# Modulation sums as f32 column-tile products with a block transpose on VectorE, and products of constants on TensorE ahead of the attention's first head

## The chip, the cores and the metric

The kernel runs on one core of a Trainium2 chip. The metric is the device time of one execution in microseconds (us). A difference under 0.3% can't be told from no change in this kernel.

## What is computed

The program is a decoder trunk of two layers over 512 tokens of 1024 channels. A conditioning vector gives nine modulation vectors per layer (a shift, a scale and a gate for each of three sublayers), and these come from a product of one row with a 1024 by 9216 matrix per layer:

```python
e = jax.nn.silu(c @ cond_w + cond_b[None, :])
for i in range(DEPTH):
    mod = (e @ ada_w[i] + ada_b[i][None, :]).reshape(B, N_SUBLAYERS, N_MOD, D_MODEL)
    shift, scale, gate = mod[:, :, 0], mod[:, :, 1], 1 + mod[:, :, 2]
    h = modulate(x, norm_g[i, 0], shift[:, 0], scale[:, 0])
    x = x + 0.5 * gate[:, 0][:, None, :] * swiglu(h, ffn_w1[i, 0], ffn_w3[i, 0], ffn_w2[i, 0])
    ...        # the mixer: a causal convolution in layer 0, stick-breaking attention in layer 1
    h = modulate(x, norm_g[i, 2], shift[:, 2], scale[:, 2])
    x = x + 0.5 * gate[:, 2][:, None, :] * swiglu(h, ffn_w1[i, 1], ffn_w3[i, 1], ffn_w2[i, 1])
```

The attention has 16 heads of 64 channels. For each head it forms logits z, a softplus of z, a sum of that over later keys, and the exponential of the difference as the weight of a value.

## The kernel before

Five engines run their own programs, written out by hand with semaphores between them. Nothing is scheduled by a planner, so the order of an engine is the order of its code. Channels lie on the 128 partitions, tokens along the free axis. A large product is exact to f32 by a split: each operand is a high part in fp32r and the low rest, and `triple` multiplies high by high, high by low and low by high (three TensorE products of 128x512). Weights arrive by DMA (issued by SyncE) in `raw`, ScalarE writes their high part to `w`, VectorE the low part, and TensorE waits on `lo_done` for each slab.

A feed-forward sublayer (`ffn`, four of them, j = 0 to 3) has an up phase of 22 slabs of 48 products, in a loop over i with two slabs (s = 0, 1) in a body, and a down phase of 16 half slabs of 33 products.

The modulation is computed in groups q of 512 columns beside this. Group 0 to 5 are done at the start. For the others, in each up body of j = 0, 1 and 2 (`Q_BODIES` says how many), VectorE multiplies eight rows of the weights by a column of the conditioning vector and adds them into `ada_acc` (`ada_half`, two halves of four). What is left is the sum of `ada_acc` over its 128 partitions, for each of its 512 columns, and the result has to lie on partitions. ScalarE copies `ada_acc` to a high part in fp32r (`up_step`, L618), GpSimd subtracts it for the low part (`acc_lows`, L485), and TensorE, at the third of eight steps of slab s = 1, runs four pairs of products (`ada_reduce_split`, L1440 and L1441) in which the accumulator is the stationary operand and a block of ones of two columns is the moving one. Five groups are summed in another way (`ada_reduce`, L1431): four f32 products of `ada_acc` itself with one column of ones. They are four behind pairs of down slabs of j = 0 and one at the end of j = 1. VectorE then takes the sum (`ada_take`, L839): it adds the bias to 128x4 numbers of PSUM and writes `mods`.

In the down phase of j = 0 VectorE accumulates too, one half for each of six down steps d, and takes three sums. Its SyncE loads of the modulation weights go into one buffer, `ada_raw`, and the loads of the down weights stand behind them in SyncE's order:

```python
for s in range(2):
    sp.wait_ge(lo_done, N_DOWN[j] + 2 * i - 1 + s)
    sp.dma_start(raw[s][:, 0:DOWN], down_in[2 * KD * j + 2 * i + s, :, :]).then_inc(raw_s[s], 16)
if hi_i == 7:
    load_ada(2 * Q_DOWN - 1 + i)          # waits until VectorE has added the half before
```

The attention follows the products for q, k and v. TensorE's last work there is to spread the heads' factors (`head_spread`, L1599 and L1600). VectorE then scales q and k (`normalise`, L1228), splits them (`split_qk`, L1261), GpSimd writes the low parts (`split_low`, L547 and L550), and TensorE can begin on `logits(0, 0)`. Its loop over heads t and pieces p runs `logits(t + 1, p)` ahead of `suffix(t, p)`, and every second head `values`. `suffix(0, 0)` waits for the softplus of the first piece, which ScalarE (L788, L792, L794) and VectorE (L1274, L1279, L1281) make from the logits.

## Time and profile before

| | |
|---|---|
| Median of 3 runs | 2084.56 us (2081.09 to 2086.46) |
| The profiled execution: its own time | 2077.22 us |
| Its span from the first to the last instruction | 2075.4 us |
| Mean granted TensorE clock | 0.986 of full |
| TensorE busy | 2014.7 us, 97% of the span |
| VectorE, ScalarE, GpSimd busy | 1112.7, 677.2 and 183.6 us |

The clock is given as a share of 2.4 GHz. An f32 product stands as two records in the trace, since TensorE passes its operand twice; one in fp32r is one record. A view of the timeline shows when each record started and how long it took; matmuls are pipelined, so their records overlap, and what one of them costs is the distance from one start to the next.

### The profile page before, as it was taken

The page shows a single profiled execution, that of the slowest core. Times are in us where ns is not written, and L with a number is a line of the kernel's source. Part 1 is how long each engine was busy: PE and PEld are TensorE (multiplying, and loading weights), DVE is VectorE, ACT ScalarE, POOL GpSimd, SP SyncE. Part 2 cuts the span into 40 slices and gives each one's busy share as a digit, 9 for nine tenths or more (in the row PEclk, how much of TensorE's full clock was granted, in tenths as well). Part 3 has the DMA queues.
Part 4 walks back from the last instruction along what each step waited for, and adds up shares of the span by engine and source line. Part 5 has one row for each costly group of instructions (what it writes and reads, how often), then busy time and mean ns, then how long its engine had stood idle before and what let it go on. Part 6 is the DMA issues. An engine that isn't in the chain of part 4 may idle for free.

```text
span 2075.4 us, 24249 instructions
## 1 busy us (share of the span) xinstructions
PE 2014.7 (97%) x9512; PEld 1650.2 (80%) x9512; DVE 1112.7 (54%) x1326; ACT 677.2 (33%) x760; POOL 183.6 (9%) x129
## 2 busy tenths in 40 slices
PE   5999999989989999999999999999999999999999
PEld 5888888766667888888788888887888777888887
DVE  7665554487887555533655533355447755333322
ACT  2423232242254322322432322233237744222211
POOL 1100000111311000001100000110011111000000
PEclk9999999999989999999999999999989999999999
DMA  8445443434422544432254422232200032222222
GB/s 328 181 163 202 177 175 137 159 105 128 129 92 102 202 184 179 188 119 95 104 203 167 177 95 84 97 127 102 82 1 1 4 119 82 100 101 101 70 98 96
DMA packets 45510, 262.19 MB, mean 126 GB/s; under 512 B 6416, under 2 KB 7056, under 8 KB 20624
## 3 DMA queue, kind: packets, MB, share of 16 engines
q1 hardware_dynamic: 42384, 257.23, 33.8%
q10 hardware_dynamic: 3072, 4.23, 0.8%
q8 instruction: 35, 0.57, 0.1%
q14 instruction: 19, 0.16, 0.0%
HBM read 250.89 MB, written 2.10 MB: 122 GB/s over the span
## 4 chain that ended last, share of the span: by engine, by line
PE 84%; DVE 8%; DMA 3%; ACT 2%; issue 2%; POOL 1%; SPq 0%; DVEq 0%; POOLq 0%; ACTq 0%
PE ps L1327 26%; PE ps L1328 25%; PE ps L1329 25%; PE ps L1669 3%; DVE w L815 2%; DMA raw<-down_d 1%; DMA stage<-ada_d 1%; PE ps L1550 1%; PE ps L1683 1%; PE ps L1348 1%; DVE act_tmp L828 1%; DVE ada_acc L828 1%; ACT h_hi L611 1%; DVE h_lo L944 1%; ACT w L567 1%
## 5 line engine op out<-in xcount | busy, mean ns | idle before, releaser
L1327 PE MATMUL ps<-h_hi,w 128*128 128x512 f32 x1648 | 647.2, 393 | 10.1 <-DVE w L980 7.2
L1328 PE MATMUL ps<-h_lo,w 128*128 128x512 f32 x1648 | 642.7, 390 | 0.0
L1329 PE MATMUL ps<-h_hi,w 128*128 128x512 f32 x1648 | 642.5, 390 | 0.0
L1327 PEld LDWEIGHTS ps<-h_hi,w 128*128 128x128 f32 x1648 | 310.3, 188 | 81.6 <-DVE w L980 8.4
L1329 PEld LDWEIGHTS ps<-h_hi,w 128*128 128x128 f32 x1648 | 310.2, 188 | 64.8
L1328 PEld LDWEIGHTS ps<-h_lo,w 128*128 128x128 f32 x1648 | 310.2, 188 | 62.9
L815 DVE TENSOR_TENSOR w<-raw,w 128x1408 fp32r<-128x1408 f32 (+1 forms) x100 | 186.4, 1864 | 236.2 <-ACT w L567 236.1
L567 ACT ACTIVATE w<-raw 128x1408 fp32r<-128x1408 f32 (+1 forms) x100 | 157.0, 1570 | 433.8 <-PE ps L1329 367.0
L1327 PE MATMUL ps<-g_hi,w 128*128 128x512 f32 x704 | 274.6, 390 | 4.0 <-DVE w L815 4.0
L1328 PE MATMUL ps<-g_lo,w 128*128 128x512 f32 x704 | 273.9, 389 | 0.0
L1329 PE MATMUL ps<-g_hi,w 128*128 128x512 f32 x704 | 273.9, 389 | 0.0
L980 DVE TENSOR_TENSOR w<-raw,w 128x2048 fp32r<-128x2048 f32 x80 | 183.3, 2292 | 79.9 <-ACT w L632 79.9
L974 DVE TENSOR_TENSOR act_tmp<-act_tmp,ps 128x512 f32<-128x512 f32 x85 | 58.4, 687 | 306.2 <-ACT act_tmp L627 306.2
L627 ACT ACTIVATE act_tmp<-ps 128x512 f32<-128x512 f32 x85 | 50.8, 598 | 436.4 <-PE ps L1329 432.2
L828 DVE SCALAR_TENSOR_TENSOR ada_acc<-ada_raw,e_col,ada_acc 128x512 f32<-128x512 f32 x224 | 171.2, 765 | 7.3 <-DMA ada_raw<-ada_d 0.5
L1327 PEld LDWEIGHTS ps<-g_hi,w 128*128 128x128 f32 x704 | 132.1, 188 | 32.9 <-DVE w L815 5.5
L1329 PEld LDWEIGHTS ps<-g_hi,w 128*128 128x128 f32 x704 | 132.1, 188 | 27.5
L1328 PEld LDWEIGHTS ps<-g_lo,w 128*128 128x128 f32 x704 | 132.1, 188 | 27.1
L632 ACT ACTIVATE w<-raw 128x2048 fp32r<-128x2048 f32 x80 | 152.1, 1901 | 0.0
L976 DVE TENSOR_TENSOR g_lo<-act_tmp,g_hi 128x512 f32 (+1 forms) x85 | 58.8, 692 | 75.6 <-ACT g_hi L629 75.6
L957 DVE SCALAR_TENSOR_TENSOR x<-ps,gt,x 128x512 f32<-128x512 f32 x48 | 35.7, 748 | 114.0 <-PE ps L1329 114.0
L485 POOL TENSOR_TENSOR parts<-ada_acc,parts 128x512 fp32r<-128x512 f32 x27 | 34.8, 1290 | 571.2 <-ACT parts L618 571.2
(213 smaller groups left out, 1908.2 us busy)
## 6 DMA issues: line engine op xcount, KB each, us to landing
raw<-up_d SPq DMA_DIRECT2D x88, 1024.0 KB, 6.3
ada_raw<-ada_d SPq DMA_DIRECT2D x64, 1024.0 KB, 4.8
raw<-down_d SPq DMA_DIRECT2D x64, 704.0 KB, 4.1
raw<-mix_d SPq DMA_DIRECT2D x28, 1024.0 KB, 4.8
stage<-ada_d SPq DMA_DIRECT2D x12, 1024.0 KB, 13.1
u_blk<-u SPq DMA_DIRECT2D x64, 64.5 KB, 2.1
u_blk<-u ACTq DMA_DIRECT2D x64, 64.5 KB, 2.1
x<-x_t_d SPq DMA_DIRECT2D x2, 1024.0 KB, 18.1
```

The costliest lines, as they stand in the source:

```text
L567: act.activation(wsp[n % 2][:, 0, 0:cols], raw[n % 2][:, 0:cols], ACT.Copy).then_inc(hi_done, 1)
L627: act.activation(tmp, pair[s][0], ACT.Silu).then_inc(silu_done, 1)
L632: act.activation(wsp[s][:, 0, :], raw[s][:, :], ACT.Copy).then_inc(hi_done, 1)
L815: dve.tensor_tensor(wsp[n % 2][:, 1, 0:cols], raw[n % 2][:, 0:cols], f32(wsp[n % 2][:, 0, 0:cols]), ALU.subtract) \
L828: dve.scalar_tensor_tensor(out=acc, in0=buf[:, k, :], scalar=w, in1=acc, op0=ALU.mult, op1=ALU.add).then_inc(ada_step, 1)
L974: dve.tensor_tensor(tmp, tmp, pair[s][1], ALU.mult).then_inc(g_full, 1)
L976: dve.tensor_tensor(g_lo[:, 2 * i + s, :], tmp, f32(g_hi[:, 2 * i + s, :]), ALU.subtract).then_inc(g_done, 1)
L980: dve.tensor_tensor(wsp[s][:, 1, :], raw[s][:, :], f32(wsp[s][:, 0, :]), ALU.subtract) \
L1327: pe.matmul(dst, a_hi_, b_hi_, start=start, stop=False, skip_group_check=True)
L1328: pe.matmul(dst, a_hi_, b_lo_, start=False, stop=False, skip_group_check=True)
L1329: return pe.matmul(dst, a_lo_, b_hi_, start=False, stop=stop, skip_group_check=True)
L1669: last = pe.matmul(zps[:, span(base, c, P * later)], con[:, 2 if later == c else 3, :], part[:, span(0, later, P * later)], start=False, s ...
```

## The change

The sum over partitions changes its operands. All 32 groups from q = 6 on now use `ada_reduce`: four f32 products in which 32 columns of ones are stationary and a quarter of `ada_acc` (128 columns, in pieces of 32) is moving. Product b writes partitions 32b to 32b + 31 of PSUM, so each uses its own 32 columns of the array. ScalarE's copy and GpSimd's subtraction fall away with their semaphores. The sum then lies along the free axis, and VectorE transposes 128x128 of PSUM in blocks of 32x32, waits for that, and adds the bias as before. The second part is `keep_clock`: 16 products of a constant with itself (128x512, fp32r) behind the last `head_spread`, and 8 ahead of `suffix(0, 0)`, written to a bank that nothing reads.

```diff
-            def acc_lows(j, n):
-                with pool.Fori(0, n) as i:
-                    pool.wait_ge(acch_done, i + (N_SPLIT[j] + 1))
-                    pool.tensor_tensor(acc_lo, ada_acc[:, :], f32(acc_hi), ALU.subtract).then_inc(accl_done, 1)
...
-                if ada and s == 0:
-                    act.wait_ge(ada_step, 8 * (Q_FFN[j] + i) + (STEP0 - 48))
-                    act.activation(acc_hi, ada_acc[:, :], ACT.Copy).then_inc(acch_done, 1)
...
+                if not isinstance(q, int) or q >= 6:
+                    dve.transpose(ada_t, ps[:, 7, 0:P]).then_inc(ada_col, 1)
+                    dve.wait_ge(ada_col, q - 5)
+                    dve.tensor_tensor(dst, ada_t.rearrange("p (n r) -> p n r", n=4)[:, :, 0], b, ALU.add) \
+                        .then_inc(mod_done, 1)
+                    return
...
-            def ada_reduce(q, acc):
+            def ada_reduce(q):
                 pe.wait_ge(ada_step, 8 * q + (STEP0 - 40))
-                for c in range(4):
-                    last = pe.matmul(ada_ps[:, 2 * c:2 * c + 1], acc[:, c * P:(c + 1) * P], ones[:, 0:1], start=True, stop=True)
-                last.then_inc(ada_sum, 1)
-
-            def ada_reduce_split(n):
-                pe.wait_ge(accl_done, n)
-                for c in range(4):
-                    at = slice(c * P, (c + 1) * P)
-                    pe.matmul(ada_ps[:, 2 * c:2 * c + 2], acc_hi[:, at], ones_r[:, 0:2], start=True, stop=False)
-                    last = pe.matmul(ada_ps[:, 2 * c:2 * c + 2], acc_lo[:, at], ones_r[:, 0:2], start=False, stop=True)
+                for b in range(4):
+                    last = pe.matmul(ada_rows[32 * b:32 * b + 32, :, :], ones[:, 0:32],
+                                     ada_acc[:, :].rearrange("p (n b r) -> p n b r", n=4, b=4)[:, :, b, :],
+                                     start=True, stop=True, skip_group_check=True)
                 last.then_inc(ada_sum, 1)
...
+            def keep_clock(n):
+                pe.wait_ge(conr_done, 1)
+                pe.wait_ge(qkn_done, 2 * KD - 2)
+                for _ in range(n):
+                    pe.matmul(ps[:, 7, :], con[:, 0, :], con[:, :, :].rearrange("p c n -> p (c n)"), start=True,
+                              stop=True, skip_group_check=True)
+
             head_spread(14)
             head_spread(15)
+            keep_clock(16)
             for p in range(2):
                 logits(0, p)
             for t in range(HEADS):
                 for p in range(2):
                     if t + 1 < HEADS:
                         logits(t + 1, p)
+                    if t == 0 and p == 0:
+                        keep_clock(8)
                     suffix(t, p)
```

How the order of instructions changes is shown at three places. The first is TensorE's in the loop body of an up phase, in slab s = 1; L1327 to L1329 (now L1315 to L1317) are a triple of the slab. Before:

```order
L1329 MATMUL ps<-h_hi,w 128x512
L1440 MATMUL ps<-ones_r,parts 128x2
L1441 MATMUL ps<-ones_r,parts 128x2
L1440 MATMUL ps<-ones_r,parts 128x2
L1441 MATMUL ps<-ones_r,parts 128x2
L1327 MATMUL ps<-h_hi,w 128x512
```

(There are four such pairs, of which two are shown.) After:

```order
L1315 MATMUL ps<-h_hi,w 128x512
L1316 MATMUL ps<-h_lo,w 128x512
L1317 MATMUL ps<-h_hi,w 128x512
L1417 ISA
L1419 MATMUL ps<-ada_acc,ones 32x128 x4
L1315 MATMUL ps<-h_hi,w 128x512
```

The place in the slab is the same. Eight products with a moving operand of two columns have become four with one of 128 columns, which read `ada_acc` and not the two parts; the row L1417 is a step of the sequencer for the wait.

The second is VectorE's in the down phase of j = 0, at d = 1: the low part of a down weight, the take, then the four steps of `ada_half`. Before:

```order
L957 SCALAR_TENSOR_TENSOR x<-ps,gt,x 128x512
L815 TENSOR_TENSOR w<-raw,w 128x1408
L839 TENSOR_TENSOR mods<-ps,vec 128x4
L825 TENSOR_SCALAR ada_acc<-ada_raw,e_col 128x512
L828 SCALAR_TENSOR_TENSOR ada_acc<-ada_raw,e_col,ada_acc 128x512 x3
```

After:

```order
L945 SCALAR_TENSOR_TENSOR x<-ps,gt,x 128x512
L797 TENSOR_TENSOR w<-raw,w 128x1408
L822 STREAM_TRANSPOSE ps<-ps 128x128
L824 TENSOR_TENSOR mods<-ps,vec 128x4
L807 TENSOR_SCALAR ada_acc<-ada_raw,e_col 128x512
L810 SCALAR_TENSOR_TENSOR ada_acc<-ada_raw,e_col,ada_acc 128x512 x3
```

The transpose stands between the low part and the take, and all that follows on VectorE is behind it.

The third is TensorE's between the last `head_spread` and the second piece of the first logits. Before:

```order
L1599 MATMUL ps<-y_hi,sel 128x512
L1600 MATMUL ps<-y_lo,sel 128x512
L1651 MATMUL ps<-con 128x128 x3
L1327 MATMUL ps<-qk_s 128x384
L1328 MATMUL ps<-qk_s 128x384
```

After:

```order
L1579 MATMUL ps<-y_hi,sel 128x512
L1580 MATMUL ps<-y_lo,sel 128x512
L1673 MATMUL ps<-con 128x512 x16
L1631 MATMUL ps<-con 128x128 x3
L1315 MATMUL ps<-qk_s 128x384
```

The 16 products of constants stand ahead of the first logits. Eight more stand between `logits(1, 0)` and `suffix(0, 0)`.

## Rows read from the trace of the kernel before

**Rows 1.** The page: TensorE's busy time, and the last chain by engine.
```profile
PE 2014.7 (97%) x9512; PEld 1650.2 (80%) x9512; DVE 1112.7 (54%) x1326; ACT 677.2 (33%) x760; POOL 183.6 (9%) x129
...
PE 84%; DVE 8%; DMA 3%; ACT 2%; issue 2%; POOL 1%; SPq 0%; DVEq 0%; POOLq 0%; ACTq 0%
```

**Rows 2.** Groups of instructions by line: busy us, mean ns, idle before.
```profile
L1441 PE MATMUL ps<-ones_r,parts 128*128 128x2 f32 x108 | 24.8, 250 | 0.0
```

**Rows 3.** Timeline of PE in an up body: start us, us.
```profile
90.51 0.39 PE L1329 MATMUL ps<-h_hi,w 128*128 128x512 f32 x1
90.73 0.17 PE L1440 MATMUL ps<-ones_r,parts 128*128 128x2 f32 x1
...
91.54 0.48 PE L1327 MATMUL ps<-h_hi,w 128*128 128x512 f32 x1
91.86 0.39 PE L1328 MATMUL ps<-h_lo,w 128*128 128x512 f32 x1
```

**Rows 4.** Timeline of PE: four f32 products of 32 columns (head sums, L1589).
```profile
1419.51 0.39 PE L1329 MATMUL ps<-h_hi,w 128*128 128x512 f32 x1
1419.82 0.62 PE L1589 MATMUL ps<-sq_qk,ind 128*32 128x512 f32 x2
...
1420.28 0.60 PE L1589 MATMUL ps<-sq_qk,ind 128*32 128x512 f32 x2
...
1420.82 0.50 PE L1327 MATMUL ps<-h_hi,w 128*128 128x512 f32 x1
1421.15 0.40 PE L1328 MATMUL ps<-h_lo,w 128*128 128x512 f32 x1
```

**Rows 5.** The chain that ended last, in the down phase of j = 0.
```profile
340.92 0.33 SPq L371
341.79 5.54 DMA raw<-down_d
```

**Rows 6.** Timeline of PE behind the second pair of down slabs of j = 0.
```profile
365.58 0.95 PE L1431 MATMUL ps<-ones,ada_acc 128*128 128x1 f32 x8
367.13 0.50 PE L1327 MATMUL ps<-g_hi,w 128*128 128x512 f32 x1 [0.60 <-DVE w L815]
```

**Rows 7.** Timeline of all engines at VectorE's first take in that phase.
```profile
335.89 2.21 POOL L472 TENSOR_TENSOR ss<-sq_tmp 128x512 f32<-128x512 f32 x1 [43.35 <-ACT sq_tmp L574]
...
336.87 0.15 DVE L839 TENSOR_TENSOR mods<-ps,vec 128x4 f32<-128x4 f32 x1
336.94 1.44 DVE L825 TENSOR_SCALAR ada_acc<-ada_raw,e_col 128x512 f32<-128x512 f32 x1
```

**Rows 8.** Timeline of DVE in an up body, behind the take.
```profile
100.62 0.69 DVE L974 TENSOR_TENSOR act_tmp<-act_tmp,ps 128x512 f32<-128x512 f32 x1 [3.37 <-ACT act_tmp L627]
```

**Rows 9.** Stretches: us, busy by engine, then PEclk, DMA share, GB/s.
```profile
1533.00:1536.00 3.00, 0.16 (x1) 0.00 (x0) 2.22 (x5) 0.75 (x1) 2.35 (x2) 0.98 0.00 0
1540.00:1563.00 23.00, 23.00 (x78) 19.36 (x78) 11.95 (x19) 13.99 (x19) 2.62 (x2) 0.50 0.00 0
1572.00:1586.00 14.00, 14.00 (x90) 11.12 (x89) 10.98 (x17) 10.86 (x15) 2.65 (x2) 1.00 0.00 1
```

**Rows 10.** Timeline of PE, ACT and DVE from the first logits on.
```profile
1536.30 0.91 PE L1651 MATMUL ps<-con 128*128 128x128 f32 x3 [3.14 <-POOL qk_s L550]
...
1539.84 0.81 ACT L788 ACTIVATE sp_abs<-ps 128x768 f32<-128x768 f32 x1 [6.10 <-PE ps L1329]
...
1543.52 0.56 DVE L1279 CAST sp_hi<-sp_abs 128x768 fp32r<-128x768 f32 x1
...
1545.02 1.65 PE L1669 MATMUL ps<-sp_hi,con 128*128 128x384 f32 x6
...
1564.74 0.96 PE L1669 MATMUL ps<-sp_hi,con 128*128 128x384 f32 x6
...
1572.99 0.95 PE L1669 MATMUL ps<-sp_hi,con 128*128 128x384 f32 x6
...
1578.80 0.62 PE L1669 MATMUL ps<-sp_hi,con 128*128 128x384 f32 x3
```

More of the change, by code:

```diff
@@ L81 @@
 Q_BODIES = [11, 11, 7, 0]
-N_SPLIT = [0, 10, 20]
 Q_DOWN = 17
@@ L108, in trunk @@
         ada_acc = sb("ada_acc", [P, GW])
-        acc_hi, acc_lo = parts[:, 0, :], parts[:, 1, :]
         fac_hi, fac_lo = parts[:, 0, :], parts[:, 1, :]
@@ L190, in trunk @@
         ada_ps = ps[:, 7, 0:8]
+        ada_rows = ps[:, 7, 0:P].rearrange("p (n r) -> p n r", n=4)
+        ada_t = ps[:, 7, P:2 * P]
         mean_row = ps[:, 7, :]
@@ L213, in trunk @@
         start_pe = sem("start_pe")
-        acch_done = sem("acch_done")
-        accl_done = sem("accl_done")
+        ada_col = sem("ada_col")
         ada_sum = sem("ada_sum")
@@ L489, in _ @@
             h_odds(0)
-            acc_lows(0, 10)
             for c in range(KD):
@@ L539, in _ @@
                 h_odds(m)
-                if m < 5:
-                    acc_lows(m - 2, min(Q_BODIES[m - 2], 10))
             def split_low(c):
@@ L611, in h_his, with up_step @@
                         act.activation(h_hi[:, c, :], t_buf(c), ACT.Identity, bias=shift).then_inc(hhi_done, 1)
-            def up_step(j, i, s, split=True, ada=False, first=None):
+            def up_step(j, i, s, split=True, first=None):
                 n = N_UP[j] + 2 * i + s
-                if ada and s == 0:
-                    act.wait_ge(ada_step, 8 * (Q_FFN[j] + i) + (STEP0 - 48))
-                    act.activation(acc_hi, ada_acc[:, :], ACT.Copy).then_inc(acch_done, 1)
                 tmp = act_tmp[:, s, :]
@@ L637, in ffn @@
                     up_step(j, 0, s, first=FFN_ENTRY[j] if s == 0 else None)
-                if nb:
-                    with act.Fori(1, min(nb + 1, 10)) as i:
-                        for s in range(2):
-                            up_step(j, i, s, ada=True)
-                if nb < 10:
-                    with act.Fori(nb + 1, 10) as i:
-                        for s in range(2):
-                            up_step(j, i, s)
+                with act.Fori(1, 10) as i:
+                    for s in range(2):
+                        up_step(j, i, s)
                 for s in range(2):
-                    up_step(j, 10, s, split=False, ada=(nb == 11))
+                    up_step(j, 10, s, split=False)
                     hi(N_DOWN[j] + s, DOWN)
@@ L1470, in up_step @@
                 pe.wait_ge(lo_done, N_UP[j] + 2 * i + s + 1)
-                reduce_ = (lambda: ada_reduce_split(N_SPLIT[j] + i)) if ada and s == 1 else None
+                reduce_ = (lambda: ada_reduce(Q_FFN[j] + i - 1)) if ada and s == 1 else None
                 two_chunks(s, pair[s], m, reduce_).then_inc(slab_done, 1)
@@ L1504, in ffn @@
                     if j == 0:
-                        ada_reduce(Q_DOWN - 1 + i, ada_acc)
+                        ada_reduce(Q_DOWN - 1 + i)
                 if j and nb == 11:
-                    ada_reduce(Q_FFN[j] + 10, ada_acc)
+                    ada_reduce(Q_FFN[j] + 10)
             pe.wait_ge(ones_done, 3)
```

## The prediction

> **What bounds the kernel now.** I read the page first. TensorE is busy for 97% of the span, and it holds 84% of the chain that ended last [rows 1]. So a microsecond taken from TensorE's own stream is worth a microsecond nearly everywhere, and work taken from ScalarE, VectorE or GpSimd is worth something only where TensorE waits for it. Next came the timeline of TensorE inside an up body, to see what a modulation sum costs there. Ordinary products of 128x512 follow each other at about 0.225 us (90.51 to 90.73 in [rows 3]). Over the sum, the start of the last ordinary product and that of the second one after it lie 1.35 us apart [rows 3], where two ordinary steps would be 0.45. A sum thus costs 0.90 us of TensorE, and TensorE does not idle ahead of it. The view by lines counts 108 products of L1441, which is 27 sums of four [rows 2].
>
> Then the down phase of j = 0, where the other form of sum stands. There the chain does not run through TensorE. It runs from VectorE's accumulation to SyncE's modulation load at 340.92 and the down weights queued behind it, which take 5.54 us to land [rows 5]; ScalarE and VectorE split them, and TensorE, which ran a sum at 365.58, still sits idle 0.60 us for the low part [rows 6]. Last came the stretches around the attention. TensorE idles 3.14 us before the first logits [rows 10], its granted clock starts to fall inside 1533 to 1536, and from 1540 to 1563 it is 0.50, that is 1.2 GHz, with TensorE busy all the time [rows 9]. From 1572 on it is 1.00, the 2.4 GHz level.
>
> **Sums, TensorE's side.** The new sum is four f32 products with 32 stationary columns each. The trace has the same shape with 512 moving columns, in the head sums [rows 4]: 1.64 us from the last ordinary start to the second one behind, less 0.45, is 1.19 us for all four. The starts of the first and the second passes are 0.46 apart, and each of those shows two of the four products: the four run side by side. A pass of 512 columns twice over at 2.4 GHz is 0.43 us of this; with 128 columns it is 0.11. Two passes save 0.64, so the new sum costs 0.55 us. Were all of the 0.46 to shrink with the columns it would be 0.50; the other end is 0.90, no better than now, if starting eight short products binds. I take 0.55, since only the columns differ from the row that I have. It saves 0.35 us each.
>
> How many count: the 27 in the up bodies, and of the five others the one behind the last down slab of j = 0 and the one that ends j = 1. The three between down slabs of j = 0 lie beside the wait of [rows 5, 6] and give nothing. That is 29 x 0.35 = 10.2 us, between 0 and 29 x 0.40 = 11.6.
>
> **Sums, the other engines.** ScalarE's copy and GpSimd's subtraction end 27 times. TensorE waited for neither [rows 3], so nothing comes from them. VectorE gains a transpose and a wait for it, 32 times. The trace shows no transpose; on 128 columns it should lie between 0.15 for 4 columns [rows 7] and 0.69 for 512 [rows 8], by columns 0.28. The take then can't start beside it, which is some 0.1 more: 0.4 together. In an up body VectorE idles 3.37 us behind that half [rows 8], which hides it; if that cover were gone, the next gated product and low weights would be late by the rest. In the down phase of j = 0 three takes stand in the chain of [rows 5]. But there the first step of the accumulation took 1.44 us, from 336.94 to 338.38, twice what an operation of 512 columns takes elsewhere [rows 8], and it ended just after GpSimd's addition, at 335.89 + 2.21 = 338.10 [rows 7]. I read that as VectorE held back by GpSimd, and a transpose ahead of it uses up this time. I take 0; the upper end is 3 x 0.4 = 1.2 us. What would be late next is SyncE's modulation load and the down weights behind it.
>
> **Products of constants.** TensorE's last spread product ends at 1536.30 - 3.14 = 1533.16 [rows 10]. The sixteen start at about 1533.3 and take 16 x 0.225 = 3.6 us, to 1536.9. That is 0.6 us later than the logits could start, and in return TensorE has not been idle. In the kernel before, the time from the first logits to `suffix(0, 0)` is 1545.02 - 1536.30 = 8.72 us at half clock; at full clock it is 4.4 to 4.9, and eight products add 1.8. So `suffix(0, 0)` starts at about 1543.3. Its operand doesn't come later: the first piece of logits took 3.54 us at half clock (1536.30 to 1539.84), so 1.8 at full, which gives 1538.7, and from there ScalarE and VectorE need 4.24 us (1539.84 to the end of L1279), which gives 1542.9 [rows 10]. A head at full clock without `values` takes 5.81 us (1572.99 to 1578.80), so `suffix(2, 0)` starts at 1543.3 + 11.6 = 1554.9. Before it started at 1564.74, and the head from there, 8.25 us to 1572.99, should take as long as it did. The gain is 9.8 us if the heads fall into step at once. I take 9.4, with ends of 8 and 10.5.
>
> **Sum.** 10.2 + 9.4 = 19.6 us. Against the profiled execution's own 2077.22 that gives 2057.6; against the median, which is 7.3 higher, 2065.0. I predict the latter.
>
> **Rivals.**
> 1. The clock gives nothing, because it falls in spite of the constants, or because it would not have fallen in many plain executions. For the first speaks that one execution shows one fall and I can't tell what holds it up; against it, that nothing longer than a fraction of a microsecond is left idle and that full-rate heads hold 1.00 [rows 9]. Price: the constants' delays, 0.6 us for the first group and 1.8 to 3.6 for the second at either level, so +0.6 to +4 there and -6 to -10 in all: 2075 to 2079.
> 2. The sums get no cheaper (0.90 each), since eight short passes are bound by their start: eight records in 0.81 us is what [rows 3] shows for full-width loads. Only the clock is gained: 2075. Against it, four passes start as two rows almost together in [rows 4].
> 3. The side that is slower: the products don't share the array when they are short. Each of eight passes would wait for its own weights and pass alone: 0.10 us for the load and short product (0.81 / 8, [rows 3]) and 0.11 for the columns, so 8 x 0.21 = 1.7, and with 0.2 at entry and exit 1.85 instead of 0.90. That is 29 x 0.95 = +27.5, less 9.4: 2103. It turns the result slower by over 0.3% from 0.90 + (9.4 + 6.3) / 29 = 1.44 us for a sum on. Against it stand the 0.46 us between passes in [rows 4], which leave nothing for loads. The Trainium skill has a rule that says this (TensorE: Matmul & The Clock Gate, Part 3, "The mechanism": weight loads run beside products in flight only where their row groups differ). The four tiles here have one row group, so by it the loads would be exposed; [rows 4] does not bear that out at 512 columns, and no row shows 128.
> 4. The transpose is far dearer than by columns. It decides only from 3.37 us plus TensorE's lead on, some 6 us; [rows 7, 8] speak against it.
>
> **How the numbers follow.** My forecast, both gains: 0.73. Rival 1: 0.12. Rival 2: 0.08. Rival 3: 0.04. Rival 4 and what I don't see: 0.03. The likeliest case by itself spans 2061 to 2068 by its terms, and somewhat more as medians of few runs differ by some microseconds. The range for 8 in 10 goes from 2057, where both terms are at their best and the sessions differ, to 2077, which takes in rival 2 and most of rival 1. Under 2078.3 is faster by 0.3%: all of the forecast, rival 2, and two thirds of rival 1, less a little for spread, is 0.87. Same is 0.08, slower 0.05.
>
> **What would show it.** Right: from the last ordinary product before a sum to the second one after it about 1.0 us instead of 1.35; up bodies shorter by 0.35; the products at L1419 starting in two groups of four; the down phase of j = 0 as long as before; granted clock 1.00 from 1533 through the first heads, and the third `suffix` some 9 us nearer to the last spread product. Wrong: eight evenly spaced starts of the sum, idle time of TensorE for the low weights in up bodies, or a stretch at 0.50 in the first heads.

## Result and the profile after

| | before | after |
|---|---|---|
| Median (range, executions) | 2082.82 us (2080.90 to 2086.46, 4) | 2060.49 us (2058.93 to 2061.88, 4) |
| Ratio, 95% interval | | 0.9891 [0.9873, 0.9908] |
| The profiled execution, its span | 2077.22, 2075.4 us | 2061.88, 2060.1 us |
| Mean granted clock of that one | 0.986 | 0.991 |
| TensorE busy | 2014.7 us | 2000.0 us |

The change makes the kernel 22.3 us faster by the medians, and 15.3 us by the two profiled executions. The difference between these two numbers is itself a finding, and the first experiment explains it.

The page of the kernel after: busy time by engine, and the last chain by engine.

```profile
PE 2000.0 (97%) x9536; PEld 1619.9 (79%) x9536; DVE 1124.3 (55%) x1358; ACT 659.9 (32%) x733; POOL 148.8 (7%) x102
...
PE 84%; DVE 8%; DMA 3%; ACT 2%; issue 2%; POOL 1%; SPq 0%; DVEq 0%; POOLq 0%; ACTq 0%
```

Nothing has changed in what bounds the kernel: the shares of the chain are those of [rows 1]. TensorE is busy for 14.7 us less, and that is nearly the whole gain of this pair. ScalarE lost 17 us of work and GpSimd 35, which no one had waited for.

The timeline of PE in an up body of the kernel after, and below it that of DVE at the take of the same body (start us, us):

```profile
90.08 0.39 PE L1317 MATMUL ps<-h_hi,w 128*128 128x512 f32 x1
90.39 0.43 PE L1419 MATMUL ps<-ada_acc,ones 128*32 128x128 f32 x8
90.75 0.50 PE L1315 MATMUL ps<-h_hi,w 128*128 128x512 f32 x1
91.09 0.39 PE L1316 MATMUL ps<-h_lo,w 128*128 128x512 f32 x1
```

```profile
93.91 0.32 DVE L822 STREAM_TRANSPOSE ps<-ps 128x128 f32<-128x128 f32 x1
94.51 0.16 DVE L824 TENSOR_TENSOR mods<-ps,vec 128x4 f32 x1 [0.27 <-DVE ps L822]
94.65 0.49 DVE L807 TENSOR_SCALAR ada_acc<-ada_raw,e_col 128x512 f32<-128x512 f32 x1
```

From the last ordinary start (90.08) to the second one behind (91.09) are 1.01 us, where [rows 3] has 1.35. Less two ordinary steps (0.45), the sum costs 0.56 us instead of 0.90. Over a whole up body a little of that is lost again in the products behind the sum: from one sum to the next are 22.35 us, where there were 22.66, so a body is 0.31 us shorter. On VectorE the transpose, the wait and the take cost 0.74 us (93.91 to 94.65), where the take alone cost 0.07 (336.87 to 336.94 in [rows 7]).

The timeline of PE from the end of the spread products, answering to [rows 10]:

```profile
1525.19 0.39 PE L1580 MATMUL ps<-y_lo,sel 128*128 128x512 f32 x1
1525.79 3.88 PE L1673 MATMUL ps<-con 128*128 128x512 f32 x16 [0.22 <-DVE qk L1216]
1529.51 0.44 PE L1631 MATMUL ps<-con 128*128 128x128 f32 x3
...
1534.33 3.49 PE L1673 MATMUL ps<-con 128*128 128x512 f32 x8
1537.62 1.10 PE L1649 MATMUL ps<-sp_hi,con 128*128 128x384 f32 x6
...
1543.58 0.96 PE L1649 MATMUL ps<-sp_hi,con 128*128 128x384 f32 x6
...
1549.39 0.96 PE L1649 MATMUL ps<-sp_hi,con 128*128 128x384 f32 x6
...
1557.64 0.95 PE L1649 MATMUL ps<-sp_hi,con 128*128 128x384 f32 x6
```

And stretches of it, answering to [rows 9] (us, busy by engine, then PEclk, DMA share, GB/s):

```profile
1531.00:1534.00 3.00, 3.00 (x17) 2.31 (x17) 0.69 (x1) 2.48 (x3) 0.00 (x0) 1.00 0.00 0
1534.00:1538.00 4.00, 4.00 (x13) 3.17 (x13) 3.72 (x6) 3.83 (x6) 0.00 (x0) 0.59 0.00 0
1538.00:1541.00 3.00, 3.00 (x19) 2.47 (x18) 1.64 (x4) 0.81 (x1) 2.11 (x2) 0.98 0.00 0
1541.00:1560.00 19.00, 19.00 (x123) 15.67 (x121) 15.61 (x24) 14.89 (x21) 3.17 (x3) 1.00 0.00 1
```

The idle 3.14 us ahead of the first logits is gone and the first logits run at the upper level. But the clock still falls, at the eight products: 0.59 over four microseconds is (1 - 0.59) x 4 / 0.5 = 3.3 us at 1.2 GHz. It is back for the heads, where [rows 9] has 0.50 over 23 us.

### The profile page after: what moved, and what is told of

The parts are those of the page before. It is cut to its first block, busy times and chain, and to the rows that moved or that the text cites. A ratio compares the mean times of both kernels' runs of the same rounds, so it can differ in the third digit from the quotient of the medians.

```text
span 2060.1 us, 24192 instructions
## 1 busy us (share of the span) xinstructions
PE 2000.0 (97%) x9536; PEld 1619.9 (79%) x9536; DVE 1124.3 (55%) x1358; ACT 659.9 (32%) x733; POOL 148.8 (7%) x102
## 4 chain that ended last, share of the span: by engine, by line
PE 84%; DVE 8%; DMA 3%; ACT 2%; issue 2%; POOL 1%; SPq 0%; DVEq 0%; POOLq 0%; ACTq 0%
PE ps L1315 26%; PE ps L1317 25%; PE ps L1316 25%; PE ps L1649 2%; DVE w L797 2%; DMA raw<-down_d 1%; DMA stage<-ada_d 1%; PE ps L1530 1%; PE ps L1663 1%; PE ps L1336 1%; DVE act_tmp L810 1%; DVE ada_acc L810 1%; DVE h_lo L932 1%; ACT h_hi L601 1%; ACT w L557 1%
## 5 line engine op out<-in xcount | busy, mean ns | idle before, releaser
L1315 PE MATMUL ps<-h_hi,w 128*128 128x512 f32 x1648 | 648.5, 393 | 10.1 <-DVE w L968 7.2
L1317 PE MATMUL ps<-h_hi,w 128*128 128x512 f32 x1648 | 642.6, 390 | 0.0
L1315 PEld LDWEIGHTS ps<-h_hi,w 128*128 128x128 f32 x1648 | 310.0, 188 | 87.3 <-issue 11.6
L1317 PEld LDWEIGHTS ps<-h_hi,w 128*128 128x128 f32 x1648 | 310.1, 188 | 65.6
L1315 PE MATMUL ps<-g_hi,w 128*128 128x512 f32 x704 | 274.6, 390 | 6.1 <-DVE w L797 6.1
L1317 PE MATMUL ps<-g_hi,w 128*128 128x512 f32 x704 | 273.9, 389 | 0.0
L1315 PEld LDWEIGHTS ps<-g_hi,w 128*128 128x128 f32 x704 | 132.1, 188 | 35.3 <-DVE w L797 7.9
L1317 PEld LDWEIGHTS ps<-g_hi,w 128*128 128x128 f32 x704 | 132.1, 188 | 27.5
L616 ACT ACTIVATE g_hi<-act_tmp 128x512 f32 (+1 forms) x85 | 53.7, 632 | 81.3 <-DVE act_tmp L962 81.3
```

The source lines that it names most:

```text
L616: act.activation(g_hi[:, 2 * i + s, :], tmp, ACT.Copy).then_inc(ghi_done, 1)
L1315: pe.matmul(dst, a_hi_, b_hi_, start=start, stop=False, skip_group_check=True)
L1317: return pe.matmul(dst, a_lo_, b_hi_, start=False, stop=stop, skip_group_check=True)
```

## Experiments

Twelve runs, in three groups of four rows, each group on its own chip with the kernel before timed in turn beside it; the medians of before were 2082.37, 2082.40 and 2082.57 us. "Clock" is the mean granted clock of an execution. Of the stretches at half clock the trace's own record of the clock gives the length; the stretches view gives the same within some tenths of a microsecond. The last column is the time in the profile from the start of the last spread product to the first `suffix` product of the fourth head, by which the clock is back in every profile. It leaves out what happens elsewhere in the same execution. In the profile of the kernel before it is 40.2 us (1532.77 to 1572.99) and in that of the kernel after 32.5 (1525.19 to 1557.64).

| Kernel | Median us (range, executions) | Ratio to before | Clock | At half clock in the attention's profile | Last spread product to fourth head |
|---|---|---|---|---|---|
| control | 2082.42 (2072.78 to 2087.10, 12) | 0.9995 [0.9978, 1.0013] | 0.980 to 0.989 | 37.5 us | 45.0 us |
| sums_only | 2072.82 (2062.30 to 2078.19, 10) | 0.9953 [0.9937, 0.9969] | 0.981 to 0.989 | 34.1 us | 43.5 us |
| pads_only | 2072.05 (2066.87 to 2079.07, 9) | 0.9956 [0.9939, 0.9973] | 0.987 to 0.993 | 20.5 us | 41.5 us |
| take_late | 2060.82 (2058.11 to 2063.20, 6) | 0.9899 [0.9881, 0.9917] | 0.990 to 0.992 | 3.4 us | 32.5 us |
| no_16 | 2063.96 (2061.70 to 2065.25, 6) | 0.9918 [0.9892, 0.9944] | 0.988 to 0.991 | 13.7 us | 35.8 us |
| no_8 | 2071.39 (2065.40 to 2072.73, 12) | 0.9955 [0.9936, 0.9974] | 0.984 to 0.988 | 30.7 us | 43.5 us |
| wide_sums | 2072.58 (2067.67 to 2078.59, 12) | 0.9960 [0.9942, 0.9978] | 0.987 to 0.993 | none | 32.4 us |
| split_early | 2062.92 (2061.27 to 2064.82, 6) | 0.9913 [0.9887, 0.9939] | 0.989 to 0.992 | 6.8 us | 34.0 us |
| same_tile | 2079.47 (2076.19 to 2091.68, 12) | 1.0004 [0.9985, 1.0024] | 0.986 to 0.992 | 6.8 us | 34.0 us |
| conv_pads | 2059.20 (2058.14 to 2059.93, 5) | 0.9889 [0.9872, 0.9906] | 0.993 | 3.4 us | 32.4 us |
| pads_13 | 2058.55 (2056.89 to 2070.90, 6) | 0.9898 [0.9873, 0.9922] | 0.987 to 0.993 | 3.4 us | 31.8 us |
| after_again | 2060.88 (2057.88 to 2065.13, 5) | 0.9892 [0.9875, 0.9910] | 0.989 to 0.992 | 6.8 us | 34.0 us |

### control

The kernel before, unaltered.

> The kernel before, unchanged, to see how its own executions scatter. Its profiled execution took 2077.2 us with a mean clock of 0.986, its plain ones 2081 to 2086; the change gained 22.3 us in the medians, but only 15.4 between the two profiled executions. Theory A: the half-clock stretch in the attention has a length that differs from execution to execution, 27 us in the profile and longer in most others. Then the executions differ in mean clock, the slow ones lie lower than 0.986 (each 0.001 of mean clock is about 2 us of stretch at the full level, 4 us at half, and costs about 2 us), and no execution gets near 2061. Theory B: the missing 7 us lie in something that the clock does not show; then executions of 2077 and of 2086 have the same mean clock.

Measured: its executions lie 14 us apart, and the time follows the clock: 2072.8 us at 0.989, 2076.4 at 0.986, 2081.6 to 2084.4 at 0.983, 2087.1 at 0.980. Its stretch of the attention:

```profile
1539.00:1576.00 37.00, 37.00 (x126) 31.17 (x127) 17.79 (x28) 19.88 (x26) 5.24 (x4) 0.50 0.00 0
```

and the fourth head's first `suffix` product:

```profile
1580.15 0.97 PE L1669 MATMUL ps<-sp_hi,con 128*128 128x384 f32 x6
```

This is the expectation's theory A. In this execution (2084.4 us) the half-clock stretch lasts 37 us, and in the one on which the prediction rests 27 [rows 9]. From the last spread product (1535.17) to the fourth head are 45.0 us, in the other 40.2, so 4.8 of the 7.2 us between the two executions lie here. This one also has a stretch of 3.4 us at half clock at 679 us that the other lacks. So the profiled execution of before was a lucky one of its kind, 5.6 us below the median of the four in the first table, and the gain by medians is larger than that of the two profiles by about as much.

### sums_only and pads_only

One part of the change each. sums_only leaves out both groups of constants:

```diff
             head_spread(15)
-            keep_clock(16)
             for p in range(2):
...
-                    if t == 0 and p == 0:
-                        keep_clock(8)
                     suffix(t, p)
```

pads_only is the kernel before with these lines and `keep_clock` added.

> The changed kernel without the 24 products of constants. By the traces the sums alone save 27 x 0.32 us in the up bodies, give back 0.9 in the down phase of j = 0, and save nothing else: -8 us against before, 0.996. Theory A says that it scatters as widely as before, since the stretch at half clock in the attention stays. A rival: the sums are worth more than their own steps (10 to 14 us), because ScalarE and GpSimd are free of 27 operations each.

> The kernel before with the 24 products of constants alone. Between the two profiled executions the stretch from the last spread product to the values of the first heads shrank by 7.8 us. Theory A: in the medians it is worth more than that, 12 to 16 us (0.992 to 0.994), and the executions lie closer together than those of before. Theory B: 8 us (0.996), as the profiles show.

Measured: 9.6 us (0.9953) and 10.3 us (0.9956) faster than before, by the medians; 20 together, where both at once give 22, a difference that is within the intervals. The sums' part is close to the predicted 10.2, and to 29 x 0.31 = 9.0 by the bodies. For the constants both theories miss: the gain lies between their two figures, and the executions lie 12 us apart, nearly as wide as those of before (14). The constants' part has two kinds of executions: six at 2066.9 to 2074.6 us with a clock of 0.990 or more, three at 2077.8 to 2079.1 with 0.987. The profiled one is of the second kind, and its timeline of PE shows a wait that the kernel after does not have:

```profile
1548.46 0.55 PE L1651 MATMUL ps<-con 128*128 128x128 f32 x3 [1.23 <-POOL qk_s L550]
```

These are the logits of head 2, and they wait 1.23 us for GpSimd's low part of the second block of q and k. Behind this wait the clock was at half for 20.5 us. In this execution the eight products ran at the upper level (2.14 us for the group, against 3.49 after), so TensorE came there earlier than GpSimd. In the kernel after the eight were slow and nothing was waited for.

### take_late

Is VectorE's longer take in the down phase of j = 0 paid for? Here the sum is taken behind the accumulation step, so that the modulation buffer comes free sooner:

```diff
                         if s == 0:
-                            ada_take(q - 1)
+                            dve.wait_ge(ada_sum, q)
                         dve.wait_ge(ada_s, 16 * (2 * q - 11 + s))
                         ada_half(q, s, ada_raw, ada_acc[:, :])
+                        if s == 0:
+                            ada_take(q - 1)
```

> The changed kernel with one step moved: in the down phase of j = 0 the take of a sum (transpose, wait, addition) stands behind the half of the accumulation that it stood ahead of, so that the modulation load and the down weights behind it are not held up by it. Before, the steps of that chain have no transpose; in the changed kernel the phase lost 0.85 us. If the three takes are the cause, this gives back 0.9 to 2 us there in the profile (the take takes 0.74 us from its start to the next operation). If the loss is contention of another kind, the phase stays as long as in the changed kernel. In the total it can barely be told: 0.9990 to 0.9995 of the changed kernel.

Measured: 2060.82 us, as the kernel after. The phase took 127.4 us (from the first to the last start of a down product) against 128.4 after and 127.5 before, but over all fourteen profiles it lies between 127.4 and 128.4, and in after_again it is 127.7. So neither the 0.85 us that the expectation calls lost nor an effect of the take's place can be told from scatter. The reason stands in the timeline of the kernel after, on POOL and DVE, answering to [rows 7]:

```profile
332.32 2.21 POOL L471 TENSOR_TENSOR ss<-sq_tmp 128x512 f32<-128x512 f32 x1 [268.01 <-ACT sq_tmp L564]
```

```profile
333.30 0.32 DVE L822 STREAM_TRANSPOSE ps<-ps 128x128 f32<-128x128 f32 x1
333.66 0.16 DVE L824 TENSOR_TENSOR mods<-ps,vec 128x4 f32<-128x4 f32 x1
333.74 1.08 DVE L807 TENSOR_SCALAR ada_acc<-ada_raw,e_col 128x512 f32<-128x512 f32 x1
334.86 2.33 DVE L810 SCALAR_TENSOR_TENSOR ada_acc<-ada_raw,e_col,ada_acc 128x512 f32<-128x512 f32 x3
```

GpSimd's addition ends at 332.32 + 2.21 = 334.53, and VectorE's first step ends 0.29 us later, at 334.82; before the step ended 0.28 us behind GpSimd's end too. From the start of the take (now of the transpose) to the second step are 1.56 us, before 1.51 [rows 7]. The first step is short by what the transpose is long. That GpSimd holds the step back, and not that the two ends fall together, is shown by take_late itself, where the step stands ahead of the transpose and so begins earlier against GpSimd:

```profile
332.79 2.21 POOL L471 TENSOR_TENSOR ss<-sq_tmp 128x512 f32<-128x512 f32 x1 [268.81 <-ACT sq_tmp L564]
```

```profile
333.77 1.52 DVE L807 TENSOR_SCALAR ada_acc<-ada_raw,e_col 128x512 f32<-128x512 f32 x1
```

It begins 0.98 us behind GpSimd's start, not 1.42, and takes 1.52 us, not 1.08; it ends at 335.29, again 0.28 us behind GpSimd's end (335.00). In all fourteen profiles the 42 such steps take 1.08 to 1.52 us and end 0.28 to 0.29 us behind GpSimd's; in the up bodies, with no GpSimd work beside it, the same step takes 0.49 us (94.65 above). The transpose beside GpSimd took 0.32 us, as elsewhere.

### no_16 and no_8

The kernel after without one of the two groups of constants.

```diff
             head_spread(15)
-            keep_clock(16)
```

```diff
-                    if t == 0 and p == 0:
-                        keep_clock(8)
                     suffix(t, p)
```

> The changed kernel without the first 16 products of constants, with the 8. TensorE then idles some 3 us ahead of the first logits, as before. If the idle time there is what lets the clock fall, this executes like the kernel with the sums alone: 2072 to 2073, mean clock 0.983 to 0.984, with the 8 products costing 1.8 us (at full clock) to 3.4 us (at half) on top. If the clock falls for what TensorE does in the first head (short products with waits between), the 8 hold it and this stays near the changed kernel's 2060.5.

> The changed kernel without the 8 products of constants ahead of the first suffix, with the 16. TensorE then idles about 2 us there until the softplus of the first head is made. If a gap of 2 us can let the clock fall, some of the executions lose 10 to 25 us at half clock and the median goes to 2062 to 2070. If the 16 do all of the work, this is the changed kernel within 1 us, and 0 to 1 us faster where the 8 ended later than the softplus did.

Measured: without the 16, 3 us slower than after by the medians; without the 8, 11 us slower. The medians are of different sessions and the intervals of no_16 and after overlap, but the profiles say the same: from the last spread product to the fourth head are 35.8 us in no_16 and 43.5 in no_8, where the kernel after has 32.5. The group of eight is worth more, although it only delays what follows. Neither expectation holds whole. In no_16 the idle time lets the clock fall, as its first case has it, but the eight end the fall and the time stays near that of the kernel after. In no_8 the median lies just above the figure of its first case, but the fall comes ahead of the gap that was to cause it. The timeline of PE and two stretches of no_16:

```profile
1526.22 0.90 PE L1631 MATMUL ps<-con 128*128 128x128 f32 x3 [3.15 <-POOL qk_s L540]
```

```profile
1530.00:1533.00 3.00, 3.00 (x9) 2.13 (x9) 1.25 (x2) 2.94 (x4) 0.00 (x0) 0.50 0.00 0
1536.00:1539.00 3.00, 3.00 (x10) 2.42 (x9) 1.41 (x4) 1.66 (x2) 1.81 (x2) 0.53 0.00 0
1539.00:1545.00 6.00, 6.00 (x40) 5.22 (x39) 3.61 (x5) 3.16 (x5) 0.83 (x1) 1.00 0.00 0
```

The idle time is back, the clock falls, the logits run at half clock; then the eight products run back to back from 1534.93 and the clock returns behind them, 13.7 us after it fell. And of no_8:

```profile
1534.41 1.65 PE L1649 MATMUL ps<-sp_hi,con 128*128 128x384 f32 x6 [1.30 <-DVE sp_hi L1267]
```

```profile
1534.00:1564.00 30.00, 29.59 (x100) 24.71 (x102) 16.68 (x27) 16.01 (x22) 5.26 (x4) 0.51 0.00 1
```

Here nothing is idle ahead of the logits (first at 1528.17), and they run at the upper level. By the trace's record the clock falls at 1532.9, among the logits of the second head. Only then `suffix(0, 0)` waits, 1.30 us for VectorE, and the stretch stays at 0.51 with TensorE busy for 29.59 of 30 us. So the wait did not begin the fall. In the kernel after the clock falls at the same place, 5.2 us after the first logits (here 4.7), with no wait at all. What differs is what follows: eight long products there, the heads' own products here. The sixteen avert the fall that came with the idle time, one comes with the logits all the same, and behind the eight it ends early. Whether the 1.30 us of idling have a part in the length of no_8's stretch these runs don't tell.

### wide_sums

The kernel after with the old f32 form of the sum (`ada_acc` stationary, one column of ones moving), so no transpose and no split either:

```diff
-                for b in range(4):
-                    last = pe.matmul(ada_rows[32 * b:32 * b + 32, :, :], ones[:, 0:32],
-                                     ada_acc[:, :].rearrange("p (n b r) -> p n b r", n=4, b=4)[:, :, b, :],
-                                     start=True, stop=True, skip_group_check=True)
+                for c in range(4):
+                    last = pe.matmul(ada_ps[:, 2 * c:2 * c + 1], ada_acc[:, c * P:(c + 1) * P], ones[:, 0:1],
+                                     start=True, stop=True)
```

> The changed kernel with another form of its sums: four f32 products with ada_acc itself stationary and one column of ones moving, and no transpose, which is the form of L1431 before. ScalarE's copy and GpSimd's subtraction stay away. It tells the shape of the products from the work taken off the other engines. Theory: the sum costs 0.90 us in this form (L1431 in the trace before), so this is 27 x 0.32 = 8.6 us slower than the changed kernel, less 1 for the transposes in the down phase of j = 0: 2068. The rival, that the gain came from freeing ScalarE and GpSimd, says 2060 to 2061.

Measured: 2072.58 us, 12 us above the kernel after, where 8 were expected; but the executions are of several kinds, with clocks from 0.987 to 0.993. The timeline of PE in an up body:

```profile
91.04 0.39 PE L1311 MATMUL ps<-h_hi,w 128*128 128x512 f32 x1
91.27 0.95 PE L1413 MATMUL ps<-ones,ada_acc 128*128 128x1 f32 x8
92.08 0.48 PE L1309 MATMUL ps<-h_hi,w 128*128 128x512 f32 x1
92.40 0.39 PE L1310 MATMUL ps<-h_lo,w 128*128 128x512 f32 x1
```

The sum costs 1.36 less 0.45, 0.91 us, as the split form, and a body takes 22.66 us, as before. At a clock of 0.990 the executions stand at 2071.7 to 2073.2 us, and those of take_late at 2062.8 to 2063.2, 9 to 10 us apart; 29 x 0.31 is 9. So the gain lies in the new form of the products, not in dropping the split or in ScalarE and GpSimd having less to do: four f32 products of 128 stationary columns cost as much as the eight in fp32r. Which part of the new form it is, same_tile tells.

### split_early

take_late, with the split of the second block of q and k made ahead of the loop over heads, against the wait that pads_only showed:

```diff
             normalise(15)
+            split_qk(1)
             for t in range(HEADS):
                 magnitude(t)
...
-                if t % 2 == 0 and t // 2 + 1 < KD:
+                if t % 2 == 0 and 1 < t // 2 + 1 < KD:
```

> take_late with one more step moved: VectorE splits the second pair of q and k ahead of the loop over heads, not behind the first head's softplus. In the kernel with the products of constants alone TensorE waited 1.23 us for GpSimd's low part of that pair at the logits of the third head, and the clock fell for 20.5 us just behind it; in the changed kernel's trace the wait did not occur, since the first head ran partly at half clock. Theory: the wait goes, so that no execution has a long half-clock stretch in the attention; the median is 0 to 2 us below take_late's 2060.8 and the worst execution stays under 2063. It can also lose: the two casts (0.84 us) and GpSimd's 2.7 us now stand ahead of the first head's softplus, up to 0.8 us.

Measured: 2062.92 us, no better than take_late (2060.82). The wait at head 2 can't occur here, and it had not occurred in take_late's profile. The expectation that the slowest execution stays under 2063 us failed (2064.82), and the profile still has 6.8 us at half clock. So that wait is not what sets the time of these kernels; what decides between 3.4 and 6.8 us is open.

### same_tile

Is the new sum cheap because its products run side by side, or only because they are short? Here all four write the same partitions, so use the same 32 columns of the array. Three quarters of each sum are lost, so the results are wrong and the times alone count (one more product, in the first up phase, fills the bank once):

```diff
-                    last = pe.matmul(ada_rows[32 * b:32 * b + 32, :, :], ones[:, 0:32],
+                    last = pe.matmul(ada_rows[0:32, :, :], ones[:, 0:32],
```

> The four f32 products of each modulation sum all write partitions 0 to 31 and so use the same 32 columns of the array; one product of constants fills the bank once, in the first up phase. Three quarters of each sum are lost (the later product overwrites the earlier one); times alone count. Theory A (the new sum is cheap because its four products run side by side in four groups of 32 columns): here they pass one after another. The sum costs at least four double passes of 128 columns, 8 x 0.053 + 0.3 = 0.75 us, and up to 1.85 us if each waits for its weights as well; I expect about 1.2, starts evenly spaced, 29 x 0.65 = 19 us slower than the changed kernel, 2080. Theory B (it is cheap only because 128 columns are few, the place in the array doesn't matter): 0.56 us as now and 2060.5.

Measured: 2079.47 us, 18.6 slower than after_again beside it. Five of its twelve executions stand at 2089.7 to 2091.7 with a clock of 0.986; the other seven, at 0.991 or 0.992, stand at 2076.2 to 2079.5, 18 us above those of after_again at 0.992 (2057.9 to 2061.0). The timeline of PE in an up body:

```profile
91.33 0.39 PE L1317 MATMUL ps<-h_hi,w 128*128 128x512 f32 x1
91.64 1.06 PE L1419 MATMUL ps<-ada_acc,ones 128*32 128x128 f32 x8
92.64 0.50 PE L1315 MATMUL ps<-h_hi,w 128*128 128x512 f32 x1
92.97 0.40 PE L1316 MATMUL ps<-h_lo,w 128*128 128x512 f32 x1
```

1.64 us less 0.45 is 1.19 for the sum, 0.63 more than in the kernel after; a body is 0.62 us longer (22.97 against 22.35), and 29 x 0.63 = 18.3. The single starts of the eight passes, from the trace's records:

```
after      90.394 90.401 90.408 90.414 | 90.528 90.534 90.541 90.548
same_tile  91.645 91.778 91.887 91.996   92.105 92.215 92.324 92.433
```

In the kernel after four start within 0.02 us and the other four 0.134 us behind. In one tile the second starts 0.133 us behind the first and each later one 0.109 behind the one before. That is the mean time of L1419's loads of 32 columns there (109 ns), and twice what 128 columns take at 2.4 GHz (0.053); which of the two sets the pace, the load or the pass itself, no run here tells. What is shown is that in four groups of columns four loads and four passes go on at once, and in one group one at a time.

The Trainium skill (TensorE: Matmul & The Clock Gate, Part 3, "The mechanism") lets a weight load run beside products only where the row groups differ. The four tiles here have one row group, and in the kernel after the second four loads begin at 90.421 to 90.441, within 0.05 us of the first products' start: the trace does not agree. It agrees with another page (TensorEngine Tiling (Array Packing), "Key Properties"), by which different tiles load and multiply in parallel.

### conv_pads

take_late, with 38 products of constants with the tokens where TensorE waits for the first block of the convolution's input:

```diff
             for c in range(KD):
                 conv_in(c)
+                if c == 1:
+                    pe.wait_ge(bias_done, 3)
+                    for _ in range(38):
+                        pe.matmul(ps[:, 7, :], ones_r[:, :], h_hi[:, 0, :], start=True, stop=True,
+                                  skip_group_check=True)
                 if c >= 1:
                     conv_taps(c - 1)
```

> As take_late, and 38 products of constants with the normalised tokens (128x512, fp32r) where TensorE idles 9 us ahead of the first convolution taps. Theory A (what helped in the attention helps here): the granted clock does not fall at 456, the 3.3 us of taps that ran at half clock take half, so -1.6 us against take_late, 2059.2. Theory B (the taps are not what is waited for, or the next wait lets the clock fall in their place): no difference, 2060.8, with a fall that starts elsewhere. Theory C (the pads end later than the taps could begin): up to 1 us slower.

Measured: 2059.20 us, 1.7 below after_again beside it, all five executions at a clock of 0.993. The timeline of PE and the stretch, of take_late first:

```profile
461.11 6.07 PE L1532 MATMUL ps<-u_blk,taps_w 128*32 128x512 f32 x40 [7.62 <-DMA u_blk<-u]
467.10 0.50 PE L1317 MATMUL ps<-h_hi,w 128*128 128x512 f32 x1
```

```profile
453.12 9.03 PE L1542 MATMUL ps<-h_hi,ones_r 128*128 128x512 f32 x38
462.07 4.50 PE L1532 MATMUL ps<-u_blk,taps_w 128*32 128x512 f32 x40
466.50 0.50 PE L1317 MATMUL ps<-h_hi,w 128*128 128x512 f32 x1
```

```profile
453.00:462.00 9.00, 9.00 (x40) 7.04 (x38) 8.87 (x12) 2.45 (x3) 0.00 (x0) 1.00 0.67 177
```

The fall is gone and the forty taps pass in 4.4 us instead of 6.0, as theory A has it. Some of it is given back, as theory C has it: the constants end 1.0 us after the taps could begin in take_late's profile (in that of the kernel after the data came at 463.05, so it varies). From the last product ahead of the wait to the first one behind the taps are 13.6 us here, 14.0 in take_late's profile and 15.5 in both of the kernel after. The gain is at best as large as a session's scatter, though in the expected place and of the expected size.

### pads_13 and after_again

Thirteen constants for sixteen in take_late (`keep_clock(13)`), and the kernel after once more.

> As take_late, with 13 products of constants ahead of the first logits in place of 16. Theory A (the first group ends later than the logits could start, and what counts is that TensorE isn't left idle): 3 x 0.225 = 0.7 us faster than take_late, 2060.1, no wait over 0.3 us before the logits, clock 1.00 there. Theory B (the number matters for the clock by itself): a half-clock stretch of 14 us or more in the first heads and 2064 to 2072.

> The changed kernel once more, unaltered, for the spread of its medians and of its stretches at half clock: 2060.5 +- 2 us, mean granted clock 0.990 to 0.992 in each execution. If its gain depended on the stretch at half clock falling luckily short, some executions would stand at 2065 or above with a clock of 0.987 or less.

Measured: 2058.55 and 2060.88 us. The timelines of PE, pads_13 first:

```profile
1523.92 3.24 PE L1675 MATMUL ps<-con 128*128 128x512 f32 x13 [0.22 <-DVE qk L1218]
1526.99 0.45 PE L1633 MATMUL ps<-con 128*128 128x128 f32 x3
```

```profile
1523.84 3.92 PE L1675 MATMUL ps<-con 128*128 128x512 f32 x16 [0.22 <-DVE qk L1218]
1527.59 0.44 PE L1633 MATMUL ps<-con 128*128 128x128 f32 x3
```

The logits come 3.07 us behind the first constant instead of 3.75, and TensorE is not left idle. So three of the sixteen were too many, 0.7 us. But one of its six executions took 2070.9 us at a clock of 0.987, as three of pads_only did, which has all sixteen. Whether fewer constants make such an execution likelier, one of six can't tell. The kernel after has stayed between 2057.9 and 2065.1 us in nine executions. conv_pads and pads_13 are the fastest medians here, by 2 us or less, which five or six executions can't settle; both together were not tried.

## Why the prediction was right

**The size of a sum.** Predicted 0.55 us for 0.90, measured 0.56. The step from 512 to 128 columns, in which two passes shrink with the columns and the rest stays, held. An up body is shorter by 0.31 us, not by the 0.35 that the prediction names as a sign. The passes start in two groups of four, as was to be seen if it is right; same_tile shows that this is what saves the time, since without it the sum costs 1.19, more than the 0.90 of the kernel before. That is rival 3's mechanism in a milder form: a sum of 0.11 us per pass and not 0.21.

**How many sums count.** 29 x 0.31 = 9.0 us, and sums_only gives 9.6 by the medians of its session; 10.2 was predicted. The steps of a sum are 0.56 us at 30 places and not 29, since only two of the three sums between down slabs of j = 0 have an idle stretch right behind them; the phase swallows that one too, see below. In the profiled pair the stages show it less clearly, because short stretches at half clock lie elsewhere in each execution: after has one at 661 us and one longer at 569, before one at 1037.

**VectorE.** Estimated 0.4 us for transpose and wait. In the loop bodies it is 0.74 - 0.07 = 0.67, since the take starts 0.28 us after the transpose's end, not 0.1; where the take stands outside a loop, as in the down phase of j = 0, it starts 0.04 us after it (333.66), and both cost 0.37 more than the take alone. The cover held in the up bodies. The transpose itself, estimated at 0.28, is 0.32 (L822: 324 ns over 32). The Trainium skill (VectorE: DVE Perf Modes, "The three transpose paths") has 311 ns for 128x128 in bf16; the 324 ns here, in f32 and from PSUM to PSUM, are 4% more. In the down phase the prediction of no loss held by the mechanism it named, VectorE's first step ending with GpSimd's addition; its comparison was only too mild, as the same step takes 0.49 us where GpSimd is idle, so 1.44 is three times that. The shorter sums gave nothing there, as predicted: TensorE's five waits for low parts in that phase add up to 6.1 us in the kernel after (5.4 in after_again), 4.0 before (4.4 in control).

**The constants: right in kind, mis-sized.** The term was 9.4 us. In the profiled pair the stretch from the last spread product to the first `suffix` of the third head shrank from 31.97 us (1564.74 less 1532.77) to 24.20 (1549.39 less 1525.19), 7.8. Two steps of the working failed, in opposite directions. First, "the granted clock 1.00 through the first heads": it fell for 3.3 us (a stretch at 0.50 in the first heads is what the prediction itself names as a sign of being wrong), so the eight products took 3.3 us (1534.33 to 1537.62) where 1.8 was the term, and `suffix(0, 0)` came 1.9 us later than the working has it. Second, the term was worked out on one execution of before, with 27 us at half clock, and applied to a median; control has 37.5 in an execution nearer the median, and from there to the kernel after the stretch up to the fourth head shrinks by 12.5 us (45.0 to 32.5), not 7.8. By medians the constants give 2072.82 - 2060.82 = 12.0 us (sums_only against take_late, both in one session), or 10.3 by pads_only. So the first error took 1.6 us from the 9.4 and the second added some 4; that the term came out only 2.6 us too small is in part luck. The whole gain was 22.3 us for 19.6, and the median of before, which had one more execution by then, lay 1.7 lower: together the 4.5 us between 2065.0 and 2060.5.

**The other rivals.** The clock gives nothing: no; without the eight, which bring it back early, 11 us are lost (no_8). That it falls in spite of the constants, as this rival has it, did happen in eight profiles, but for 3.4 or 6.8 us where the eight stood. The sums get no cheaper: no. The transpose is far dearer: no, 0.67 us with the wait, of 3.37.

## What to carry to other kernels

Take the price of a small product from a row of the same tiling, and scale only the part that goes with the columns: that gave 0.55 us for a measured 0.56. Where the granted clock is a term, one profiled execution is not enough: compare its own time with the median and look at several, since a stretch at half clock differs by 10 us from one execution to the next. And ask of constants in a wait not only whether they keep the clock up, but where the next fall lies and what ends it: here the group that cost time and filled only 1.3 us was worth more than the one that filled 3 us.

## What the runs showed that was not expected

- A fall of the clock came without idle time. In eight profiles, of seven kernels with constants ahead of the logits, it falls 3.5 to 5.3 us after the first logits, and no wait over 0.22 us stands between the spread products and that. In two (pads_only, wide_sums) it does not fall there. Between, TensorE runs mostly products of 64 rows and 128 to 512 columns. What in them lets the clock fall was not found.
- A stretch at half clock does not end soon though TensorE is counted busy: with the attention's own products it lasted 20.5 to 37.5 us in five profiles, of four kernels. Behind eight products of 128x512 back to back it ended in all eight profiles that have both: in seven after 3.4 or 6.8 us, and in no_16, 13.7 us after the fall, as the eight ended.
- A wait of 1.23 us at the logits of head 2 was followed by a stretch of 20.5 us in pads_only, and by none at the same instruction in wide_sums. What decides between the two was not found.
- Four f32 products of 128 columns in four groups of array columns cost 0.56 us together, and in one group 1.19.
- VectorE's step `TENSOR_SCALAR` that begins beside GpSimd's addition ends 0.28 us behind it, wherever it begins (1.08, 1.44 or 1.52 us long, 0.49 without GpSimd).
- VectorE's wait for its own transpose costs 0.25 us or more in a loop body (0.27 at 94.51), where the value waited for depends on the loop's index, and 0.03 to 0.04 where it is a number of the program. That the index makes the difference was not tested.
